# Attention scores on all 128 rows of TensorE in a two-layer decoder trunk, with four stages and the merge end in another order

## The chip, the cores and the metric

One core of a Trainium2 chip runs the whole program in one launch. The metric is the device time in microseconds of one execution. An execution with the profiler on is shown beside the timed ones.

## The reference

Two layers over `x` (512 tokens, 1024 channels), then an RMSNorm. In each layer `h = rmsnorm(x)` is projected once, and the columns are shared by three token mixers:

```python
...
scale = Dh ** -0.5
...
s = jnp.einsum('bqhd,bkhd->bhqk', qi, k, preferred_element_type=jnp.float32) * scale
s = s + ci[..., None] - c_keys[:, :, None, :]
...
prob = jax.nn.softmax(jnp.where(mask, s, NEG), axis=-1)
...
```

These lines are branch A (8 heads of 64, forget bias `c`, no rotation). Branch B has 8 rotated query heads that share 2 key groups, with a compressed, a selected (`sel`) and a window (`win`) part. Branch C has 4 heads of two rotated 64-wide maps each, whose probabilities are subtracted, and values of 128. Every branch result is gated, projected to 1024 channels, merged by sigmoid gates computed from `h`, projected once more and added to `x`. A gated per-layer embedding `p` is added last. Everything is float32.

## The kernel before

**Data.** Channels lie on partitions, tokens along the free axis. `hybrid_trunk` works through *tiles*: a tile is one projection of 128 output columns over 512 tokens. A float32 product is made of three products in a fast 32-bit format: `w_hi h_hi`, `w_lo h_hi`, `w_hi h_lo`, with `hi` the rounded value and `lo` the rest. `dense` (L732 to L734) issues these three for each k step of 128 channels. `hidden` (L745, L746) is the same for the compression tiles `w1k`, `w1v`, with two products of 256 columns a step and four steps a tile. For each tile ScalarE makes `w_hi` from `raw` (L1033) and VectorE `w_lo` (L1262). There are two buffers for them, four for `raw`, and two PSUM banks `D`: a tile can start only when the tile two before it is evacuated.

**Scores.** A stage handles one unit `u` (two heads, or two maps of a head) for the four query blocks `i`; its scores have `(i + 1) * 128` key columns. Stages 0 to 3 are branch A, 4 to 7 branch B (`sel` and `win`), 8 to 11 branch C. A head is 64 wide, so a pair of heads fills 128 partitions, head 0 on partitions 0 to 63, head 1 on the others. Item `S` makes both heads' scores in banks `Sc[0]` and `Sc[1]`:

```python
for step, (qx, kx) in enumerate(((q_hi[b], ka), (q_lo[b], ka), (q_hi[b], kb))):
    last = step == 2 and m != "a"
    for h in range(2):
        ps = slice(HD * h, HD * h + HD)
        ins = pe.matmul(Sc[h][:, 0:n], qx[ps, qs], kx[ps, 0:n], start=(step == 0), stop=last)
```

These are L879. In branch A one more product per head adds the forget bias from `ck` with the selector `selr` (L885). VectorE adds the mask and takes the maximum (L1514), ScalarE the exponential (L1148). Then TensorE transposes (`T`, L898) into `Tr`, one engine copies to `pT` (L540, L542), and TensorE multiplies with the values (`V`, L920). `N` normalizes on VectorE. In branch C `CB` combines the two maps, and `SQ`, `MS`, a power on POOL and `YN` make an RMS norm. `Y` transposes the unit's result (L936), and `YS` splits it into `y_hi` and `y_lo`.

**Queries and keys.** `qa` and `ka` go from the bank to high and low parts in the `arena` by one ScalarE copy (L1100) and one VectorE instruction (L1406), each on 128 partitions. `qb`, `ksb`, `kwb`, `qc`, `kc` are rotated: a copy to `qf` or `rx`, four DMAs that swap halves into `rs`, a product with the sine on POOL (`rs` to `rb`, L684), a product with the cosine, and at item `rot` the sum (L1503), the high part on ScalarE (L1141) and the low part on VectorE (L1505). `kcb` and `vcb` are laid out as `flat` for the `w1` tiles; `ht`, `kcmp`, `vcmp` finish the compression.

**Order.** `make_schedule` writes one list of items, and each engine walks through its share of it in that order. `dense_tiles` says by hand which tiles belong to which stage, and within a stage the k steps are spread evenly over the ticks of the attention work; some items follow a tile by a fixed count of steps (`rot` by 11, `ht` by 4). SP walks through the list too: its one DMA queue loads weights six tiles ahead and does the swaps. After stage 11 come 8 pairs `mgc`, `brc` (the merge), whose sums in `acc` are split into `h_hi` (L1173) and `h_lo` (L1605). Six parts are split ahead of the evacuation of the last `brc`, two behind it. Then come 8 tiles `out`, then `gate` and `ple`.

Of the kernel before, what the change touches and what calls it, by code (L numbers as in the profile page):

```python
# [32 lines left out]
P = 128  # L33
HD = 64
# [89 lines left out]
def make_schedule(NQ):  # L124
# [37 lines left out]
    def emit_group(g):  # L162
# [4 lines left out]
        if k == steps(kind) - 1:  # L167
# [13 lines left out]
            if kind == "w1k" and tiles[t][1] == 3:  # L181
                follow.extend([[4, ("ht", t)], [7, ("kcmp", t)]])
            if kind == "w1v" and tiles[t][1] == 3:
                follow.extend([[4, ("ht", t)], [7, ("vcmp", t)]])
# [88 lines left out]
def hybrid_trunk(nc, x, p, positions, norm_g, w_in, b_forget, cmp_pe_k, cmp_w1_k, cmp_b1_k, cmp_w2_k,  # L273
# [24 lines left out]
    for it in items:  # L298
# [14 lines left out]
        elif it[0] == "T":  # L313
            (pt_act if it[1] % 2 and branch(prob_rows[it[1]][0]) == "B" else pt_dve).add(it[1])
        elif it[0] == "YS":
            ysplit.add(it[1])
    DA0 = NM
# [11 lines left out]
    EARLY = 6  # L329
# [50 lines left out]
    with ctx:  # L380
# [21 lines left out]
        at_arena = -(-nc.sbuf_base // 32) * 32  # L402
        arena = sb("arena", [P, 16 * S], F32R)
        vbd = nc.alloc_sbuf_tensor_at("vbd", [P, 2, P], F32, offset=at_arena + 12 * S * 4)
# [3 lines left out]
        q_hi, q_lo = [part(0), part(1)], [part(2), part(3)]  # L408
        k_hi, k_lo = [part(4), part(5)], [part(6), part(7)]
        ks_hi, ks_lo, kw_hi, kw_lo = part(8), part(9), part(10), part(11)  # L410
# [17 lines left out]
        rb = sb("rb", [P, S])  # L428
# [24 lines left out]
        kcmpT = sb("kcmpT", [P, 2 * C32])  # L453
        cs_ = sb("cs_", [P, NQ, 2, C32])
# [8 lines left out]
        diag = rb  # L463
# [20 lines left out]
        def f(ap):  # L484
# [21 lines left out]
                 "act_flat").split()  # L506
        once = "nm_s npow_s diag_s pe_norm pe_rb lam_s act_lam lf_s p_ld zero_s xn_s vz_s va_step h2_hi_s h2_lo_s".split()
# [36 lines left out]
        def kind_of(t):  # L544
            if t < T0:
                return tiles[t][0]
            if t < T1:
                return ("mgc", "brc")[(t - T0) % 2]
# [9 lines left out]
        def rot_dst(kind, n):  # L558

            if kind == "ksb":  # L560
                return ks_hi, ks_lo, None
            if kind == "kwb":
                return kw_hi, kw_lo, None
            u = (4 if kind == "qb" else 8) + n
            return (k_hi[u % 2], k_lo[u % 2], u) if kind == "kc" else (q_hi[u % 2], q_lo[u % 2], u)

        with nc.Block() as block:

            @block.sync
            def _(sp):  # L570
# [12 lines left out]
                for L in range(DEPTH):  # L583
# [8 lines left out]
                    def static_load(t):  # L592
# [4 lines left out]
                        load(L, kind_of(t), tiles[t][1] if t < T0 else (t - T0) // 2 if t < T1 else t - T1 if t < T2 else (t - T2) // 2, t)  # L597
# [24 lines left out]
                    for it in items:  # L622
                        if it[0] == "end" and tiles[it[1]][0] in ROTATED:
# [4 lines left out]
                            if n > 1:  # L628
                                sp.wait_ge(M["pool_rot"], n - 1)
                            for a, b in ((0, 32), (32, 0), (64, 96), (96, 64)):  # L630
                                sp.dma_start(rs[a:a + 32, :], src[b:b + 32, :]).then_inc(M["sw_ld"], 16)  # L631
                        if it[0] == "end" and it[1] + 6 < T0 + 4:
                            static_load(it[1] + 6)

# [12 lines left out]
            def _(pool):  # L647
# [8 lines left out]
                pool.memset(halfs[:], -0.5).then_inc(i_const, 1)  # L656
                pool.memset(kcmpT[:], 0.0).then_inc(i_const, 1)
                pool.memset(f(ck[:]), 0.0).then_inc(i_const, 1)
                pool.wait_ge(i_const, 9)
# [5 lines left out]
                for n, r in enumerate((0, 32, HD, HD + 32)):  # L665
                    pool.affine_select(out=self_[:], in_=self_[:], compare_op=ALU.not_equal, fill=1.0, base=-r,
                                       pattern=[[-1, 8]], channel_multiplier=1).then_inc(i_const, 1)
                    pool.wait_ge(i_const, 12 + n)
                pool.tensor_copy(selr[:], self_[:]).then_inc(i_const, 1)
                for L in range(DEPTH):  # L670
# [5 lines left out]
                    for it in items:  # L676
                        if it[0] == "swap":
# [4 lines left out]
                            if n > 1:  # L682
                                pool.wait_ge(M["dve_rs"], n - 1)
                            pool.tensor_tensor(rb[:], rs[:], sinT[:], ALU.mult).then_inc(M["pool_rot"], 1)  # L684
                        if it[0] == "ht" and tiles[it[1]][0] == "w1v":
                            pool.wait_ge(M["pe_dense"], it[1] + 1)
# [1040 lines left out]
```

## Time and profile before

| | us |
|---|---|
| median of 3 runs | 1562.36 |
| lowest, highest | 1562.06, 1563.16 |
| profiled execution, its own time | 1562.81 |
| its span on the core | 1561.0 |
| TensorE busy (7957 products) | 1502.1 |
| VectorE busy | 941.8 |
| ScalarE busy | 638.4 |
| POOL busy | 74.0 |
| DMA | 129.47 MB, mean 83 GB/s |

The span is the time from the first to the last instruction of the core; the execution has 1.8 us more around it. Busy time is the union of the records of an engine, so overlapping products are counted once. A line of the profile names the source line, engine, operation, what is written and what is read. An idle time before a group is put down to the instruction that ended it. The second layer repeats the first one's pattern from about 768 us on.

### The profile page before, as it was taken

To read this page: it belongs to the slowest core of one execution; us is meant where nothing else is said; L and a number is where in the kernel's file an instruction comes from. 1 tells how busy PE (TensorE), PEld (TensorE's weight loads), DVE (VectorE), ACT (ScalarE), POOL (GpSimd) and SP (SyncE) were. 2 spreads that over 40 slices of the span, in tenths; PEclk is the share of its full clock that TensorE was granted. 3 is DMA by queue.
4 is the path that set the end of the run, shared out by engine and by line. 5 is a ranking of instruction groups with operands and counts; after the bars stand their busy time and mean duration, and the time that the engine had idled before them with its cause. 6 is when DMAs were issued, how large, how long until landed. Compare 5 with 4: busy or idle time off the path is not lost.

```text
span 1561.0 us, 22645 instructions
## 1 busy us (share of the span) xinstructions
PE 1502.1 (96%) x7957; PEld 1205.9 (77%) x7957; DVE 941.8 (60%) x2205; ACT 638.4 (41%) x1492; POOL 74.0 (5%) x80
## 2 busy tenths in 40 slices
PE   8999999999999999999999999999999999999997
PEld 6777777887787777878787777787887777788785
DVE  6866665555556766455576657655555666754544
ACT  6533434333344434343444334334333443433343
POOL 1000000000000000000200000000000000000011
PEclk9999999999999999999999999999999999999998
DMA  7223322222223332331342324222222333233222
GB/s 195 81 82 88 96 66 63 62 68 61 68 62 94 92 79 78 94 112 58 112 112 68 102 68 109 71 54 66 62 62 74 80 83 88 68 96 106 81 82 74
DMA packets 250299, 129.47 MB, mean 83 GB/s; under 512 B 45690, under 2 KB 245972, under 8 KB 250196
## 3 DMA queue, kind: packets, MB, share of 16 engines
q1 hardware_dynamic: 250196, 128.13, 30.8%
q8 instruction: 60, 0.98, 0.3%
q14 instruction: 43, 0.35, 0.1%
HBM read 118.67 MB, written 2.10 MB: 77 GB/s over the span
## 4 chain that ended last, share of the span: by engine, by line
PE 79%; DVE 9%; issue 5%; ACT 4%; DMA 1%; POOL 1%; SPq 1%; ACTq 0%; DVEq 0%; POOLq 0%
PE D L732 21%; PE D L734 19%; PE D L733 19%; PE Ob L920 7%; PE S L879 4%; PE T L898 3%; DVE w_lo L1262 2%; ACT w_hi L1033 1%; ACT probs L1148 1%; DMA rs<-rx 1%; PE Mb L936 1%; SPq L631 1%; DVE h_lo L1605 1%; PE Mb L846 1%; PE Ob L924 1%
## 5 line engine op out<-in xcount | busy, mean ns | idle before, releaser
L732 PE MATMUL D<-h_hi,w_hi 128*128 128x512 f32 x1264 | 543.1, 430 | 17.2 <-DVE zs L1410 4.8
L734 PE MATMUL D<-h_lo,w_hi 128*128 128x512 f32 x1264 | 496.5, 393 | 0.0
L733 PE MATMUL D<-h_hi,w_lo 128*128 128x512 f32 x1264 | 494.5, 391 | 0.0
L1262 DVE TENSOR_TENSOR w_lo<-raw,w_hi 128x512 fp32r<-128x512 f32 (+2 forms) x504 | 297.2, 631 | 313.7 <-ACT w_hi L1033 313.4
L1033 ACT ACTIVATE w_hi<-raw 128x512 fp32r<-128x512 f32 (+2 forms) x504 | 266.3, 575 | 313.9 <-PE D L734 313.0
L732 PEld LDWEIGHTS D<-h_hi,w_hi 128*128 128x128 f32 x1264 | 238.6, 189 | 78.1 <-issue 20.6
L1148 ACT ACTIVATE probs<-probs,nmax 128x128 f32<-128x128 f32 (+3 forms) x256 | 141.9, 555 | 366.7 <-DVE nmax L1514 366.7
L734 PEld LDWEIGHTS D<-h_lo,w_hi 128*128 128x128 f32 x1264 | 237.5, 188 | 53.0
L733 PEld LDWEIGHTS D<-h_hi,w_lo 128*128 128x128 f32 x1264 | 239.5, 189 | 30.7 <-issue 0.5
L1514 DVE CUSTOM_DVE_ANT_0 probs<-S,maskb 128x128 f32<-128x128 f32 (+3 forms) x256 | 115.1, 486 | 51.1 <-PE S L879 30.3
L542 DVE COPY pT<-T 128x128 f32<-128x128 f32 (+3 forms) x160 | 77.4, 486 | 50.1 <-PE T L898 49.6
L920 PEld LDWEIGHTS Ob<-v_b,pT 128*128 128x128 f32 x640 | 90.5, 190 | 12.3 <-ACT pT L540 1.9
L898 PE MATMUL T<-ident,probs 128*128 128x128 f32 x560 | 97.9, 273 | 1.7 <-ACT probs L1148 1.7
L879 PE MATMUL S<-arena 64*128 64x384 f32 (+3 forms) x768 | 93.8, 349 | 0.9 <-DVE arena L1406 0.9
L732 PE MATMUL D<-y_hi,w_hi 128*128 128x512 f32 x224 | 94.0, 420 | 0.4 <-DVE y_lo L1600 0.4
L898 PEld LDWEIGHTS T<-ident,probs 128*128 128x128 f32 x560 | 72.3, 140 | 28.0 <-ACT probs L1148 5.4
L879 PEld LDWEIGHTS S<-arena 64*128 64x128 f32 x768 | 57.0, 185 | 45.6 <-issue 41.3
L734 PE MATMUL D<-y_lo,w_hi 128*128 128x512 f32 x224 | 87.9, 393 | 0.0
L733 PE MATMUL D<-y_hi,w_lo 128*128 128x512 f32 x224 | 87.5, 390 | 0.0
L920 PE MATMUL Ob<-v_b,pT 128*128 128x64 f32 x640 | 85.4, 264 | 0.3
L684 POOL TENSOR_TENSOR rb<-rs,sinT 128x512 f32<-128x512 f32 x28 | 36.2, 1292 | 970.0 <-DMA rs<-rx 588.3
L920 PEld LDWEIGHTS Ob<-v_ac,pT 128*128 128x128 f32 x480 | 67.0, 192 | 16.1 <-DVE pT L542 8.9
(241 smaller groups left out, 1496.8 us busy)
## 6 DMA issues: line engine op xcount, KB each, us to landing
raw<-in_w_in_dram SPq DMA_DIRECT2D x124, 512.0 KB, 3.9
raw<-in_w_in_dram SPq DMA_DIRECT2D x32, 256.0 KB, 3.7
raw<-in_w_out_dram SPq DMA_DIRECT2D x16, 512.0 KB, 4.0
raw<-in_w_ple_gate_dram SPq DMA_DIRECT2D x16, 512.0 KB, 4.2
rs<-rx SPq DMA_DIRECT2D x80, 64.0 KB, 2.0
raw<-in_cmp_w_k_dram SPq DMA_DIRECT2D x8, 512.0 KB, 3.7
raw<-in_cmp_w_v_dram SPq DMA_DIRECT2D x8, 512.0 KB, 3.7
raw<-in_w_br_a_dram SPq DMA_DIRECT2D x16, 256.0 KB, 2.9
```

Of the source, the lines that this page charges most:

```text
L542: eng.tensor_copy(pT[:, k % 2, 0:n], Tr[k % 2][:, 0:n]).then_inc(M["pt_dve_s"], 1)
L684: pool.tensor_tensor(rb[:], rs[:], sinT[:], ALU.mult).then_inc(M["pool_rot"], 1)
L732: pe.matmul(o, w_hi[:, sl, cs], hi[:, k, :], start=(k == 0), stop=False)
L733: pe.matmul(o, w_lo[:, sl, cs], hi[:, k, :], start=False, stop=False)
L734: ins = pe.matmul(o, w_hi[:, sl, cs], lo[:, k, :], start=False, stop=last)
L879: ins = pe.matmul(Sc[h][:, 0:n], qx[ps, qs], kx[ps, 0:n], start=(step == 0), stop=last)
L898: ins = pe.transpose(Tr[k % 2][:, j * P:(j + 1) * P], src[:, j * P:(j + 1) * P], ident[:])
L920: ins = pe.matmul(Ob[:, oc], pT[:, k % 2, j * P:(j + 1) * P], vs(j), start=(j == 0), stop=(j == i))
L1033: A(w_hi[:, sl, half], raw[:, ring(L, t, RAW), half], ACT.Copy).then_inc(M["act_hi"], 1)
L1148: A(probs[:, r % NP_, 0:n], probs[:, r % NP_, 0:n], ACT.Exp, scale=-1.0, bias=nmax[:, r % 8:r % 8 + 1], accum_out=sums[:, u % 2, i, c:c + ...
L1262: TT(w_lo[:, sl, half], raw[:, ring(L, t, RAW), half], f(w_hi[:, sl, half]), ALU.subtract).then_inc(M["dve_lo"], 1)
L1514: dve.tensor_tensor_reduce(probs[:, r % NP_, 0:n], Sc[r % 2][:, 0:n], maskb[:, S - n:S], -1.0, 3.0e38, ALU.add, ALU.min, nmax[:, r % 8:r % ...
```

## The change

*Scores.* Queries and keys get another layout. For each head the stationary operand holds its high part on one half of the partitions and its low part on the other half (`q_st`). The moving operand holds the same key part on both halves, once for the high part and once for the low part (`k_hi`, `k_lo`, a set per key tile). A head's scores are two products on 128 rows, `q_st x k_hi` and `q_st x k_lo`. That adds `q_lo k_lo` to the three products of before. In branch A a third product with `selr` and `ck` on 128 rows follows. Head 0 comes first, then head 1, each with its own wait for `dve_max`.

*Making the layout.* Each evacuation and each rotation writes its high and its low part in two instructions of 64 partitions and 512 columns, in place of one of 128 partitions. Key parts are written on one half and copied to the other by two DMAs of 256 KB per key tile (10 key tiles per layer, semaphore `kd_s`). SP issues them, for `ka` at the tile's end and for the rotated ones at item `rot`, and waits there for VectorE. Scores wait for `kd_s`. `rb` is gone: POOL multiplies `rs` in place, and SP waits for `dve_rs` of the rotation before, not `pool_rot`, ahead of the swap. `vbd` has a place of its own and is cleared once.

*Stages -1 to 3.* The tiles stand in another order, and `ht` and `kcmp`/`vcmp` follow after 12 and 16 steps.

*Merge end.* The last four tiles are `mgc 6`, `mgc 7`, `brc 6`, `brc 7`; three `h` parts are split ahead of the sum of `brc 6`, five behind that of `brc 7`.

```diff
--- before.py
+++ after.py
...
-    st = {-1: [("va", 0), ("va", 1), ("va", 2), ("va", 3), ("fg", 0), ("qa", 0), ("ka", 0), ("qa", 1)]}
+    st = {-1: [("va", 0), ("va", 1), ("va", 2), ("va", 3), ("fg", 0), ("ka", 0), ("qa", 0), ("qa", 1)]}
     st[0] = [("kcb", 0), ("ka", 1), ("za", 0), ("w1k", 0)]
-    st[1] = [("qa", 2), ("ka", 2), ("w1k", 1), ("ksb", 0), ("w1k", 2), ("za", 1)]
-    st[2] = [("qa", 3), ("w1k", 3), ("ka", 3), ("za", 2), ("vcb", 0)]
-    st[3] = [("qb", 0), ("w1v", 0), ("kwb", 0), ("w1v", 1), ("za", 3), ("w1v", 2), ("vsb", 0), ("w1v", 3), ("vwb", 0)]
+    st[1] = [("qa", 2), ("w1k", 1), ("ka", 2), ("w1k", 2), ("za", 1), ("w1k", 3), ("vcb", 0)]
+    st[2] = [("qa", 3), ("w1v", 0), ("ka", 3), ("w1v", 1), ("za", 2), ("w1v", 2), ("qb", 0)]
+    st[3] = [("w1v", 3), ("ksb", 0), ("za", 3), ("kwb", 0), ("vsb", 0), ("vwb", 0)]
...
+        q_st = [[part(6 * b + h) for h in range(2)] for b in range(2)]
+        k_at = [2, 8, 12]
+        k_hi = [[part(a + 2 * h) for h in range(2)] for a in k_at]
+        k_lo = [[part(a + 2 * h + 1) for h in range(2)] for a in k_at]
+        KS, KW = 0, 2
...
                             if n > 1:
-                                sp.wait_ge(M["pool_rot"], n - 1)
+                                sp.wait_ge(M["dve_rs"], n - 1)
...
+                            if kind == "ka":
+                                sp.wait_ge(M["dve_evac"], dve_evac.after(it[1]))
+                            else:
+                                sp.wait_ge(M["qk_s"], rots.after(it[1]))
+                            if kdup.after(it[1]) > 1:
+                                sp.wait_ge(M["kd_s"], 32 * (kdup.after(it[1]) - 1))
+                            for h in range(2):
+                                both = part(k_at[k_set(kind, n)] + 2 * h, 2)
+                                sp.dma_start(f(both[half(1 - h), :]), f(both[half(h), :])).then_inc(M["kd_s"], 16)
...
+                            for h in range(2):
+                                if r >= 2:
+                                    pe.wait_ge(M["dve_max"], r - 1 + h)
+                                qx = q_st[b][h][:, i * P:n]
+                                pe.matmul(Sc[h][:, 0:n], qx, k_hi[ks][h][:, 0:n], start=True, stop=False)
+                                ins = pe.matmul(Sc[h][:, 0:n], qx, k_lo[ks][h][:, 0:n], start=False, stop=m != "a")
+                                if m == "a":
+                                    hh = 2 * u + h
+                                    ins = pe.matmul(Sc[h][:, 0:n], selr[:, hh:hh + 1].to_broadcast([P, P]), ck[:, 0:n],
+                                                    start=False, stop=True)
+                                ins.then_inc(M["pe_s"], 1)
...
-                                dst = (q_hi if kind == "qa" else k_hi)[n % 2]
-                                A(dst, D[:], ACT.Copy, scale=QSCALE if kind == "qa" else 1.0).then_inc(M["act_evac"], 1)
+                                dst = (q_st if kind == "qa" else k_hi)[n % 2]
+                                for h in range(2):
+                                    ins = A(dst[h][half(h), :], D[half(h), :], ACT.Copy, scale=QSCALE if kind == "qa" else 1.0)
+                                ins.then_inc(M["act_evac"], 1)
...
-                            A(hi_, rc[:], ACT.Copy).then_inc(M["act_rot"], 1)
...
+                            for h in range(2):
+                                ins = A(dst[h][half(h), :], rc[half(h), :], ACT.Copy)
+                            ins.then_inc(M["act_rot"], 1)
...
+                    lo(T1 - 2)
+                    lo(T1 - 1)
+                    for m in range(3):
                         merged_lo(m)
+                    merged_last(0)
+                    lo(T1)
+                    merged_last(1)
+                    for m in range(3, NM):
+                        merged_lo(m)
+                    lo(T1 + 1)
...
```

Where instructions stand. TensorE, a score group of 384 columns in stage 4 (`D` dense products, `S` scores, `T` transpositions), before:

```order
L733 MATMUL D<-h_hi,w_lo 128x512
L734 MATMUL D<-h_lo,w_hi 128x512
L879 MATMUL S<-arena 128x384 x6
L732 MATMUL D<-h_hi,w_hi 128x512
L733 MATMUL D<-h_hi,w_lo 128x512
L734 MATMUL D<-h_lo,w_hi 128x512
L898 MATMUL T<-ident,probs 128x128 x2
```

and now:

```order
L744 MATMUL D<-h_hi,w_lo 128x512
L745 MATMUL D<-h_lo,w_hi 128x512
L892 MATMUL S<-arena 128x384
L893 MATMUL S<-arena 128x384
L892 MATMUL S<-arena 128x384
L893 MATMUL S<-arena 128x384
L743 MATMUL D<-h_hi,w_hi 128x512
L744 MATMUL D<-h_hi,w_lo 128x512
L745 MATMUL D<-h_lo,w_hi 128x512
L910 MATMUL T<-ident,probs 128x128 x2
```

Six products on 64 rows, which one row counts together, became four on 128 rows; what is around them stands where it stood.

VectorE in stage 1, from the end of tile `ka 2` on, with a `w1` tile behind it on TensorE (`w_lo` are low weights, `arena` is the key's low part, `tmp` a `w1` tile's sum, `ISA probs` the mask and maximum), before:

```order
L1262 TENSOR_TENSOR w_lo<-raw,w_hi 128x512 x2
L1406 SCALAR_TENSOR_TENSOR arena<-D,arena 128x512
L1560 RECIPROCAL coef<-sums 128x2
L1561 TENSOR_TENSOR y_q<-Ob,coef 128x128
L1262 TENSOR_TENSOR w_lo<-raw,w_hi 128x512 x2
L1428 TENSOR_TENSOR tmp<-D,tmp 64x256
L1429 TENSOR_TENSOR tmp<-D,tmp 64x256
L1514 ISA probs,nmax<-S,maskb 128x384
```

and now:

```order
L1297 TENSOR_TENSOR w_lo<-raw,w_hi 128x512 x2
L1445 SCALAR_TENSOR_TENSOR arena<-D,arena 64x512 x2
L1604 RECIPROCAL coef<-sums 128x2
L1605 TENSOR_TENSOR y_q<-Ob,coef 128x128
L1558 ISA probs,nmax<-S,maskb 128x384
L1558 ISA nmax 128x1
L1558 ISA probs,nmax<-S,maskb 128x384
L1558 ISA nmax 128x1
L548 COPY pT<-T 128x256
```

The evacuation into `arena` is two instructions of 64 partitions; scores now stand ahead of the next low weights and the `w1` sum (`tmp`), which came first before.

VectorE in stage 9, between the combination of two maps and the norm of the unit before (`rc` and `arena` are the rotation of `qc 2`, `msq` and `y_q` the items `MS` and `YN`), before:

```order
L1528 SCALAR_TENSOR_TENSOR probs<-probs,coef 128x256
L1503 TENSOR_TENSOR rc<-rc,rb 128x512
L1505 TENSOR_TENSOR arena<-rc,arena 128x512
L542 COPY pT<-T 128x128
L1578 TENSOR_SCALAR msq<-msq 128x4
L1582 TENSOR_TENSOR msq<-msq 128x4
L1583 TENSOR_TENSOR msq<-msq 128x4
L1584 TENSOR_SCALAR msq<-msq 128x4
L1585 TENSOR_TENSOR msq<-msq 128x4
L1586 TENSOR_TENSOR y_q<-y_q,msq 128x512
```

and now:

```order
L1572 SCALAR_TENSOR_TENSOR probs<-probs,coef 128x256
L1540 TENSOR_TENSOR rc<-rc,rs 128x512
L1545 TENSOR_TENSOR arena<-rc,arena 64x512 x2
L548 COPY pT<-T 128x128
L1622 TENSOR_SCALAR msq<-msq 128x4
L1626 TENSOR_TENSOR msq<-msq 128x4
L1627 TENSOR_TENSOR msq<-msq 128x4
L1628 TENSOR_SCALAR msq<-msq 128x4
L1629 TENSOR_TENSOR msq<-msq 128x4
L1630 TENSOR_TENSOR y_q<-y_q,msq 128x512
```

The rotation stands where it stood, right ahead of `MS`, and its last step is two instructions.

## Rows read from the trace of the kernel before

**Rows 1.** The page, busy time, share of the span and instructions of each engine.
```profile
PE 1502.1 (96%) x7957; PEld 1205.9 (77%) x7957; DVE 941.8 (60%) x2205; ACT 638.4 (41%) x1492; POOL 74.0 (5%) x80
```

**Rows 2.** The waits: engine, line, releaser: us in total, times, longest us.
```profile
PEld D L732 <- DVE w_lo L1262: 14.1, 12, 2.5
PE Mb L936 <- DVE y_q L1586: 7.4, 6, 1.3
PE Mb L819 <- DVE tmp L1432: 4.6, 2, 2.3
```

**Rows 3.** The timeline, PE, around a score group of 512 columns, branch B.
```profile
315.67 0.40 PE L734 MATMUL D<-y_lo,w_hi 128*128 128x512 f32 x1
315.99 0.97 PE L879 MATMUL S<-arena 64*128 64x512 f32 x6
316.89 0.50 PE L732 MATMUL D<-h_hi,w_hi 128*128 128x512 f32 x1
317.23 0.40 PE L733 MATMUL D<-h_hi,w_lo 128*128 128x512 f32 x1
317.47 0.40 PE L734 MATMUL D<-h_lo,w_hi 128*128 128x512 f32 x1
```

**Rows 4.** The same, around groups of 384, 256 and 128 columns.
```profile
301.82 0.40 PE L734 MATMUL D<-h_lo,w_hi 128*128 128x512 f32 x1
303.21 0.39 PE L733 MATMUL D<-h_hi,w_lo 128*128 128x512 f32 x1
1173.02 0.40 PE L734 MATMUL D<-h_lo,w_hi 128*128 128x512 f32 x1
1174.23 0.40 PE L733 MATMUL D<-h_hi,w_lo 128*128 128x512 f32 x1
450.87 0.40 PE L734 MATMUL D<-y_lo,w_hi 128*128 128x512 f32 x1
452.02 0.39 PE L733 MATMUL D<-h_hi,w_lo 128*128 128x512 f32 x1
```

**Rows 5.** The timeline around tile `w1k 1`: PE, then ScalarE, then VectorE.
```profile
107.39 0.40 PE L734 MATMUL D<-h_lo,w_hi 128*128 128x512 f32 x1
107.62 0.28 PE L745 MATMUL D<-w_hi,arena 128*128 128x256 f32 x1
108.46 0.28 PE L746 MATMUL D<-w_lo,arena 128*128 128x256 f32 x1
110.59 0.47 PE L732 MATMUL D<-h_hi,w_hi 128*128 128x512 f32 x1 [0.96 <-DVE arena L1406]
108.94 0.58 ACT L1100 ACTIVATE arena<-D 128x512 fp32r<-128x512 f32 x1
109.77 0.68 DVE L1406 SCALAR_TENSOR_TENSOR arena<-D,arena 128x512 fp32r<-128x512 f32 x1
```

**Rows 6.** The timeline, PE: transpositions of 128 columns, two and three together.
```profile
303.67 0.38 PE L898 MATMUL T<-ident,probs 128*128 128x128 f32 x2
305.73 0.49 PE L898 MATMUL T<-ident,probs 128*128 128x128 f32 x3
```

**Rows 7.** The timeline, PE, at the end of the merge, seventh k step of `out 0`.
```profile
684.34 0.50 PE L732 MATMUL D<-h_hi,w_hi 128*128 128x512 f32 x1 [1.47 <-DVE h_lo L1605]
```

**Rows 8.** The timeline, PE, in stage 3, behind tile `w1v 2`.
```profile
197.75 0.47 PE L732 MATMUL D<-h_hi,w_hi 128*128 128x512 f32 x1 [2.31 <-DVE zs L1410]
```

**Rows 9.** A stretch: busy PE, PEld, DVE, ACT, POOL; then granted clock, DMA share, GB/s.
```profile
187.00:230.00 43.00, 39.86 (x229) 32.25 (x228) 26.71 (x69) 13.78 (x36) 1.61 (x2) 0.96 0.36 86
```

**Rows 10.** The timeline, ScalarE and PE, behind the rotation of `qb 1`.
```profile
243.19 0.36 ACT L540 ACTIVATE pT<-T 128x256 f32<-128x256 f32 x1
243.45 0.40 PE L734 MATMUL D<-h_lo,w_hi 128*128 128x512 f32 x1
243.68 0.58 PE L920 MATMUL Ob<-v_b,pT 128*128 128x64 f32 x4
```

**Rows 11.** The page, DMA issues: count, KB each, us to landing.
```profile
raw<-in_w_in_dram SPq DMA_DIRECT2D x32, 256.0 KB, 3.7
```

More of the change, by code:

```diff
@@ L316, in hybrid_trunk @@
             ysplit.add(it[1])
+    kdup = Count()
+    for it in items:
+        if it[0] == "end" and tiles[it[1]][0] == "ka" or it[0] == "rot" and tiles[it[1]][0] in ("ksb", "kwb", "kc"):
+            kdup.add(it[1])
     DA0 = NM
@@ L453, in hybrid_trunk @@
         kcmpT = sb("kcmpT", [P, 2 * C32])
+        vbd = sb("vbd", [P, 2, P])
         cs_ = sb("cs_", [P, NQ, 2, C32])
@@ L546, in kind_of @@
                 return tiles[t][0]
+            if t >= T1 - 4 and t < T1:
+                return ("mgc", "mgc", "brc", "brc")[t - T1 + 4]
             if t < T1:
@@ L633, in _ @@
                             static_load(it[1] + 6)
+                        if it[0] in ("end", "rot") and it[1] in kdup.order and (tiles[it[1]][0] == "ka") == (it[0] == "end"):
+                            kind, n, _ = tiles[it[1]]
+                            if kind == "ka":
[7 more added lines that the diff above has]
+                                sp.dma_start(f(both[half(1 - h), :]), f(both[half(h), :])).then_inc(M["kd_s"], 16)
                     sp.wait_ge(M["dve_ysplit"], 12)
@@ L681, in _ @@
                             pool.wait_ge(M["sw_ld"], 64 * n)
[L682 to L686, printed above, removed]
-                            pool.memset(vbd[:], 0.0).then_inc(M["vz_s"], 1)
+                            pool.tensor_tensor(rs[:], rs[:], sinT[:], ALU.mult).then_inc(M["pool_rot"], 1)
                         if it[0] == "MS":
@@ L882, in _ @@
-                            if m == "a":
-                                for h in range(2):
-                                    ps, hh = slice(HD * h, HD * h + HD), 2 * u + h
-                                    pe.matmul(Sc[h][:, 0:n], selr[ps, hh:hh + 1].to_broadcast([HD, P]), ck[ps, 0:n],
-                                              start=False, stop=True).then_inc(M["pe_s"], 1)
+                                    if u == 4:
+                                        pe.wait_ge(M["kd_s"], 32 * kdup.after(tile_of[("ksb", 0)]))
+                                elif u == 4:
+                                    pe.wait_ge(M["kd_s"], 32 * kdup.after(tile_of[("kwb", 0)]))
@@ L1605, in merged_lo @@
                         STT(h_lo[:, m, :], acc[:, m, :], 0.5, f(h_hi[:, m, :]), ALU.mult, ALU.subtract).then_inc(M["dve_merge"], 1)
-                    def merge_tiles(i, m0, last):
+                    with dve.Fori(0, NM // 2 - 1) as i:
                         for j in range(4):
-                            t = T0 + 2 * m0 + j
-                            if last and j == 3:
-                                for m in range(EARLY):
-                                    merged_lo(m)
+                            t = T0 + j
```

167 lines of the change are left out of this document (91 added, 76 removed).

## The prediction

> **What bounds the kernel now.** I read the busy times first: TensorE is busy for 96% of the span, VectorE for 60%, ScalarE for 41% [rows 1]. So an instruction taken off TensorE is worth its full time wherever TensorE is not waiting, and an instruction added on VectorE or ScalarE costs nothing until TensorE has to wait for it. Second, the waits: TensorE's are short and have few causes [rows 2]. It waits for VectorE's `y_q` before a `Y` transposition (7.4 us in 6 waits), for `tmp` before `ht` (4.6 us), and for low weight parts (14.1 us). Third, the timeline of TensorE around a score group. Records of products overlap, so the price of anything there is a distance between starts, not a recorded length: `D` products of 512 columns start 0.23 to 0.24 us apart and are recorded as 0.40 us long [rows 3].
>
> **The score products.** Before, a group is six products on 64 rows, the two heads in pairs. At 512 columns the last `D` before it starts at 315.67, the six scores at 315.99, the next `D` at 316.89 and the one after at 317.23 [rows 3]. From 315.67 to 317.23 is 1.56; two `D` distances are 0.46; so the group costs 1.10 us. Three rounds of 0.23 are only 0.69 of that. The rest is an entry gap (0.32 instead of 0.23) and a longer exit (0.33, then 0.34 to the next product). The pairs do run side by side: six products of 512 columns in 0.90 us is faster than one after the other. The same reckoning gives 0.93 at 384 columns (303.21 - 301.82 - 0.46), 0.75 at 256 (1174.23 - 1173.02 - 0.46) and 0.69 at 128 (452.02 - 450.87 - 0.46) [rows 4].
>
> After, a group is four products on 128 rows, one behind the other. At 512 columns I take the `D` distance, 0.23. At 256 columns the eight products of a `w1` tile start at 107.62 to 108.46, seven distances of 0.12 [rows 5]. At 128 columns the third transposition adds 0.49 - 0.38 = 0.11 [rows 6]. For 384 I take the value between, 0.17. That makes 0.92, 0.69, 0.48 and 0.44, if nothing is lost on entry or exit because `D` and `S` now are products of one shape and type. The gain is 0.18, 0.24, 0.27 and 0.25 per group. Of the 24 groups at 128 columns in branches B and C, 18 are followed by the compressed products, their transpositions or `V` and not by `D`; the long exit is not in their price, so I take 0.17 as their mean. Branches B and C have 24 groups of each width in both layers: (0.18 + 0.24 + 0.27 + 0.17) x 24 = 20.6 us. Branch A has 8 of each, with the `ck` row: one more round before, two more products now, so each gains one distance less: (0.25 - 0.11) + (0.27 - 0.12) + (0.24 - 0.17) + (0.18 - 0.23) = 0.31, x 8 = 2.5 us. **Together -23.1 us** on TensorE.
>
> The Trainium skill has two rules here. "TensorEngine Tiling (Array Packing)", Key Properties, says that changing the tiling mode drains the engine. By it the entry and exit gaps belong to the 64-row form and go with it; the trace agrees so far as it can, 0.32 into a score group against 0.23 from `D` to `V` [rows 3, 10]. The same list says that different tiles load and multiply in parallel; by that alone the change gives up concurrency, and that is a rival below.
>
> **Merge end.** The stall before the seventh k step of the first `out` tile, 1.47 us [rows 7], is `h_lo` part 6 standing on VectorE behind the low weights of `out 1` and the sum and add of the last `brc`. Now `mgc 6, mgc 7, brc 6, brc 7` leaves the sum of channel group 6 to run beside `brc 7`, and only that of 7 and five `h_lo` parts behind it. There VectorE has a fused sum and an add (about 1.3 us at 0.6 to 0.7 each) and the five parts at 0.7; TensorE has the transpositions of `p` (about 1 us) and eight k steps of 0.68. Part 7 is ready about 5.5 us behind `brc 7`, its k step due at 5.8. I count -1.7 us per layer, **-3.4**. Bounds: -4.0 (the stall and its short successor) and +1 (the second `out` tile's weights, split last, come late).
>
> **Stages 0 to 3.** `ht` moves 8 steps later: its 4.6 us of wait [rows 2] go. Tiles `w1` no longer stand behind a `rot`; the 2.31 us wait for `zs` [rows 8] and, I assume, one like it in the second layer, 4.6 together, shrink to about 0.3 each. But a `w1` tile is short, and the tile behind it needs the bank of the tile before it. Before, `ka 2` and `qa 3` stand so. There from the last product at 107.39 ScalarE copies at 108.94, VectorE subtracts at 109.77, and `D` goes on at 110.59, 3.2 us later [rows 5]. After, `qa 2`, `ka 2`, `qa 3` and `ka 3` all stand so, and both copies are in halves: half the partitions, the same 512 columns. I price a second half a little under the recorded 0.58 and 0.68 [rows 5], since records overlap: 0.5 on ScalarE and 0.6 on VectorE, so 4.3 us, of which `w1`, scores and one transposition cover 2.1 to 2.5: 2.2 + 1.8 us twice per layer, 8.0, beside 1.7 for the other `w1` tiles, 9.7 per layer, 19.4. Before it is 4.6 + 4.6 + about two thirds of the 14.1 for `w_lo` [rows 2], an estimate, 18.6. In the stretch with the 2.31 us wait TensorE's granted clock is 0.96 in the mean of 43 us [rows 9], so 1.7 us more were lost, which need not return. **Net -1**; bounds -12 (all short-tile waits vanish) and +8 (each is 1 us longer).
>
> **What the halves add.** 8 evacuations and 14 rotations per layer have a second ScalarE and a second VectorE half. Most are hidden beside `D` tiles of 5.5 us. Three places are not.
> - Behind the rotations of `qb 1` to `qb 3` and `qc 0`, ScalarE's copy of `pT` ends at 243.55 and `V` starts at 243.68 [rows 10]: no slack. A half more on ScalarE, 0.5, and scores that are 0.1 to 0.2 shorter ahead of it give 0.6 each, 8 times: +4.8.
> - Ahead of `MS` and `YN` in stages 9 and 10 the rotation of `qc` stands right before `MS` on VectorE, as the order shown above has it, and TensorE waits up to 1.3 for `y_q` [rows 2]. There the halves add 0.5 + 0.6, and the scores in between shorten by 0.24: +1.3 each, 4 times: +5.2.
> - At the start of stage 0 VectorE is the late one; two evacuations in halves less one copy of `ck` give +1.4 in the first layer and +0.5 in the second. In stage 11 and at transpositions that wait for the exponentials, the shorter scores only lengthen the wait: +2.
> **Together +13.9.** Bounds 0 and 28 (twice each).
>
> **The new transfers.** 40 DMAs of 256 KB copy each key half to the other half. A load of that size lands in 3.7 us [rows 11]. Between the end of a key tile and its first scores lie at least 3.4 us of `D` (for `kwb`, whose scores come two ticks later) and mostly 9 us and more, so I cost them at nothing; SP's waits for `qk_s` stand behind VectorE work that its next load waits for anyway. Should one be late, it is 1 to 3 us in a layer. POOL's product now overwrites `rs`, and SP waits for `dve_rs` before the next swap: the previous rotation's sum is 1 to 2 tiles old by then, cost nothing. `vbd` and `ck` save one memset and one copy.
>
> **Sum.** -23.1 - 3.4 - 1 + 13.9 = -13.6, from the profiled execution's 1562.8 us to 1549.2; its time is 0.45 us over the median, so I say **1549**.
>
> **Rivals.**
> - *Rows lost.* If the gaps around a score group come from its waits and its change of bank and not from the 64-row form, they stay, and each group has one more product time, in branch A two: (0.11 + 0.12 + 0.17 + 0.23) x (24 + 2 x 8) = 25.2 us more; with merge end and stages as above and 5 us of new waits left, 1562.4 + 25.2 - 4.4 + 5 = **1588**. It decides where the distance from `D` into `S` stays at 0.32. Against it: `V` also waits for a semaphore and changes the bank, and comes 0.23 behind `D` [rows 10]. Chance 0.1. By the skill's rule on independent tiles it would be this.
> - *Eaten up.* The halves cost twice what I take: 28 us, **1563**, within noise of before. For it: VectorE and ScalarE each work through one list in the order written, so an engine late at one place is late at the next, and VectorE's 60% [rows 1] is a mean. Chance 0.15.
> - *Slack holds.* VectorE and ScalarE take the halves where they idle, and the chains start earlier because scores end earlier: no new waits, **1535**. Chance 0.2. For it: ScalarE is 41% busy [rows 1].
> - The forecast, 1542 to 1556: chance 0.55.
>
> A difference under 0.2%, 3.1 us, is what a measurement of this kernel can hardly tell from none. Faster by more: 0.55 + 0.2 + a third of 0.15, 0.80. Within: 0.07. Slower: the first rival and the tail of the second, 0.13. The range holds all but that rival and the far tails: 1533 to 1566.
>
> **What would show it.** Steps right: the four score products start 0.23 apart at 512 columns, 0.32 is nowhere, and the first `D` behind a group is 0.23 before the second. The wait for `h_lo` and for `tmp` is gone; those for the evacuated `arena` and for `y_q` are longer. Wrong: score products of 128 columns more than 0.15 apart (weight loads of 128 rows not hidden); any wait of scores for a DMA; a wait for `y_q` no longer than before.

## The result and the profile after

The changed kernel takes 1576.63 us (median of 4 runs, 1576.19 to 1578.43), the kernel before 1562.76 beside it. The ratio is 1.0089, with a 95% interval of 1.0072 to 1.0107: **slower by 13.9 us**. The forecast was 13 us faster; the time lies outside the range.

The page of the changed kernel, busy times, the shares of the chain of waits, and the heaviest groups:

```profile
PE 1491.4 (95%) x7701; PEld 1245.1 (79%) x7701; DVE 974.8 (62%) x2247; ACT 668.7 (42%) x1536; POOL 73.5 (5%) x77
...
PE 74%; DVE 12%; ACT 7%; issue 5%; POOL 0%; DMA 0%; SPq 0%; ACTq 0%; DVEq 0%; POOLq 0%
...
L743 PE MATMUL D<-h_hi,w_hi 128*128 128x512 f32 x1264 | 538.9, 426 | 22.0 <-DVE arena L1445 10.2
...
arena<-arena SPq DMA_DIRECT2D x40, 256.0 KB, 3.6
```

Against [rows 1] TensorE is busy for 10.7 us less although the span is 13.4 longer (1574.4 us). In the chain PE fell from 79% to 74%, VectorE rose from 9% to 12% and ScalarE from 4% to 7%. TensorE did less and waited more.

TensorE's longest waits (us in total, times, longest):

```profile
PE Mb L948 <- DVE y_q L1630: 14.1, 6, 3.0
PE D L743 <- DVE arena L1445: 10.2, 6, 2.3
PE D L743 <- DVE arena L1442: 7.9, 4, 2.2
PE T L910 <- ACT probs L1179: 7.5, 12, 0.9
PE Ob L932 <- DVE pT L548: 7.0, 8, 1.8
...
PE Ob L932 <- ACT pT L546: 5.1, 6, 0.9
PE Mb L830 <- DVE y_f L1639: 3.0, 2, 1.8
```

`y_q` was 7.4 in six waits, 1.3 at most [rows 2]; now 14.1, up to 3.0. `arena` (evacuations of `ka`, `qa`) and the waits for ScalarE's `probs` and `pT` are new at this size. The wait for `tmp`, 4.6 in two [rows 2], is back under another name before the same `ht` transposition: 3.0 in two. There is no wait of `S` for a transfer.

The score group of 512 columns, TensorE's timeline, branch B:

```profile
318.66 0.39 PE L745 MATMUL D<-y_lo,w_hi 128*128 128x512 f32 x1
318.88 0.39 PE L892 MATMUL S<-arena 128*128 128x512 f32 x1
319.11 0.39 PE L893 MATMUL S<-arena 128*128 128x512 f32 x1
319.34 0.39 PE L892 MATMUL S<-arena 128*128 128x512 f32 x1
319.56 0.39 PE L893 MATMUL S<-arena 128*128 128x512 f32 x1
319.79 0.39 PE L743 MATMUL D<-h_hi,w_hi 128*128 128x512 f32 x1
320.02 0.39 PE L744 MATMUL D<-h_hi,w_lo 128*128 128x512 f32 x1
```

The starts are 0.22 to 0.23 us apart throughout. From the last `D` before the group to the second `D` behind it are 1.36 us; less two `D` distances the group costs 0.90 to 0.91 (1.10 before [rows 3]). The forecast said 0.92. The 0.32 is gone.

Stages 9 and 10 show the loss. The timeline of VectorE, ScalarE and TensorE of the changed kernel around `y_q` in stage 10:

```profile
555.49 0.69 DVE L1540 TENSOR_TENSOR rc<-rc,rs 128x512 f32<-128x512 f32 x1
557.57 1.39 DVE L1545 TENSOR_TENSOR arena<-rc,arena 64x512 fp32r<-64x512 f32 x2 [1.39 <-ACT arena L1171]
558.88 0.28 DVE L548 COPY pT<-T 128x128 f32<-128x128 f32 x1
559.18 0.17 DVE L1622 TENSOR_SCALAR msq<-msq 128x4 f32<-128x4 f32 x1
...
561.27 0.69 DVE L1630 TENSOR_TENSOR y_q<-y_q,msq 128x512 f32<-128x512 f32 x1
...
556.26 1.27 ACT L1171 ACTIVATE arena<-rc 64x512 fp32r<-64x512 f32 x2 [1.42 <-issue]
...
558.76 0.39 PE L745 MATMUL D<-h_lo,w_hi 128*128 128x512 f32 x1
562.10 1.08 PE L948 MATMUL Mb<-ident,y_q 128*128 128x128 f32 x4 [2.96 <-DVE y_q L1630]
```

and the same place in stage 9 by windows (busy PE, its instructions, granted clock, DMA share, GB/s):

```profile
501.00:514.00 13.00, 13.00 (x68) 1.00 0.32 83
514.00:518.00 4.00, 1.33 (x7) 0.97 0.26 65
518.00:521.50 3.50, 3.16 (x10) 0.55 0.01 4
```

The same instructions of the kernel before, in stage 10:

```profile
552.01 0.68 DVE L1503 TENSOR_TENSOR rc<-rc,rb 128x512 f32<-128x512 f32 x1
552.78 0.63 ACT L1141 ACTIVATE arena<-rc 128x512 fp32r<-128x512 f32 x1 [1.42 <-issue]
553.45 0.69 DVE L1505 TENSOR_TENSOR arena<-rc,arena 128x512 fp32r<-128x512 f32 x1 [0.75 <-ACT arena L1141]
556.33 0.69 DVE L1586 TENSOR_TENSOR y_q<-y_q,msq 128x512 f32<-128x512 f32 x1
557.16 0.63 PE L936 MATMUL Mb<-ident,y_q 128*128 128x128 f32 x4 [1.32 <-DVE y_q L1586]
```

Two halves take 1.27 us on ScalarE and 1.39 on VectorE, where one instruction of 128 rows took 0.63 and 0.69: half the partitions, the same time. VectorE waits 1.39 for ScalarE's two and then does its own two. From the rotation's sum to `y_q` it is 5.78 us (555.49 to 561.27) where it was 4.32 (552.01 to 556.33), 1.46 more, and TensorE's wait is 2.96 instead of 1.32. Behind such a wait TensorE can run for 3.4 us at 1.2 GHz instead of 2.4, as here in stage 9. In the body of the program (25 us to 1515 us) there is one such stretch before and there are seven after, 23.9 us in all. At half clock each costs half its length, 1.7 us: 11.9 instead of 1.7. The Trainium skill, "TensorE: Matmul & The Clock Gate", Terms, reckons the penalty as throttled time times one minus the clock's share, which is this half; a run below agrees.

### The profile page after: what moved, and what is told of

Read it like the earlier page. It is cut to its first block, busy times and chain, and to the rows that moved or that the text cites. A ratio compares the mean times of both kernels' runs of the same rounds, so it can differ in the third digit from the quotient of the medians.

```text
span 1574.4 us, 22204 instructions
## 1 busy us (share of the span) xinstructions
PE 1491.4 (95%) x7701; PEld 1245.1 (79%) x7701; DVE 974.8 (62%) x2247; ACT 668.7 (42%) x1536; POOL 73.5 (5%) x77
## 4 chain that ended last, share of the span: by engine, by line
PE 74%; DVE 12%; ACT 7%; issue 5%; POOL 0%; DMA 0%; SPq 0%; ACTq 0%; DVEq 0%; POOLq 0%
PE D L743 20%; PE D L745 19%; PE D L744 19%; PE Ob L932 6%; PE T L910 3%; DVE w_lo L1297 3%; ACT w_hi L1057 2%; PE S L893 2%; ACT probs L1179 2%; PE S L892 2%; ACT arena L1171 1%; ACT arena L1125 1%; DVE probs L1558 1%; DVE arena L1442 1%; PE Mb L948 1%
## 5 line engine op out<-in xcount | busy, mean ns | idle before, releaser
L743 PE MATMUL D<-h_hi,w_hi 128*128 128x512 f32 x1264 | 538.9, 426 | 22.0 <-DVE arena L1445 10.2
L698 POOL TENSOR_TENSOR rs<-rs,sinT 128x512 f32<-128x512 f32 x28 | 36.5, 1304 | 1006.3 <-DMA rs<-qf 589.5
L892 PE MATMUL S<-arena 128*128 128x128 f32 (+3 forms) x256 | 78.5, 316 | 2.3 <-DVE arena L1442 2.3
L893 PE MATMUL S<-arena 128*128 128x128 f32 (+3 forms) x256 | 80.2, 322 | 0.0
```

The source lines that it names most:

```text
L743: pe.matmul(o, w_hi[:, sl, cs], hi[:, k, :], start=(k == 0), stop=False)
L892: pe.matmul(Sc[h][:, 0:n], qx, k_hi[ks][h][:, 0:n], start=True, stop=False)
L893: ins = pe.matmul(Sc[h][:, 0:n], qx, k_lo[ks][h][:, 0:n], start=False, stop=m != "a")
```

## The experiments

Times are medians; a difference from the kernel before is what the ratio makes of 1562.8 us, one between two other kernels is that of their medians, which were not measured side by side. Where a stage is spoken of, its first score product is laid beside the same one of another trace.

**e1_merge.** The kernel before with the new end of the merge alone.

```diff
+            if t >= T1 - 4 and t < T1:
+                return ("mgc", "mgc", "brc", "brc")[t - T1 + 4]
```

> The kernel before with the merge end alone in the new order. My theory, that the halves of evacuations and rotations and the clock dips behind their waits ate the gain, has this part as it was forecast: 3 to 4 us faster, 1559, the wait for h_lo gone. The rival theory that a reordered end gives its gain back at the next tiles expects 0 to 1 us.

1560.19 us, ratio 0.9982 (0.9972 to 0.9992): -2.8. The wait for `h_lo` is gone; each layer ends about 2 us earlier against its stage 11, while this trace has two stretches at half clock where the kernel before has one. The term -3.4 holds.

**e2_order.** The kernel before with the new order of stages -1 to 3 and the later `ht` and `kcmp`, `vcmp`.

```diff
-    st[1] = [("qa", 2), ("ka", 2), ("w1k", 1), ("ksb", 0), ("w1k", 2), ("za", 1)]
+    st[1] = [("qa", 2), ("w1k", 1), ("ka", 2), ("w1k", 2), ("za", 1), ("w1k", 3), ("vcb", 0)]
-                follow.extend([[4, ("ht", t)], [7, ("kcmp", t)]])
+                follow.extend([[12, ("ht", t)], [16, ("kcmp", t)]])
```

> The kernel before with the new order of stages -1 to 3 and the later ht, kcmp and vcmp alone, without halves. My theory: the waits for tmp and for zs go and the bank waits behind four query and key tiles cost 1 us each as they do now: 3 us faster (0 to 6). The rival theory, that the order itself is what costs (stages 0 to 3 of the changed kernel are 5 us behind before when the shorter scores are counted), expects 4 to 8 us slower.

1552.34, ratio 0.9936 (0.992 to 0.9953): **-10**. The expectation had 0 to 6, its rival the other sign: both missed. By the start of stage 4 it is 7.2 us ahead in the first layer (211.2 against 218.3) and 4.7 more in the second. Counted from start to start, TensorE's waits over 0.3 us in stages 0 to 3 are 22.0 us in both layers before and 12.0 here. The one stretch at half clock, in stage 3, is gone too; another in stage 11 of the second layer takes that back. TensorE behind the short tiles `w1k 1` and `w1k 2`:

```profile
103.47 0.47 PE L732 MATMUL D<-h_hi,w_hi 128*128 128x512 f32 x1 [0.88 <-DVE arena L1408]
113.15 0.47 PE L732 MATMUL D<-h_hi,w_hi 128*128 128x512 f32 x1 [0.53 <-DVE arena L1408]
```

With undivided evacuations these waits are 0.9 and 0.5, and the `ht` transposition, which waited for `tmp`, has none. In the changed kernel the same two are

```profile
106.93 0.47 PE L743 MATMUL D<-h_hi,w_hi 128*128 128x512 f32 x1 [2.19 <-DVE arena L1442]
119.50 0.47 PE L743 MATMUL D<-h_hi,w_hi 128*128 128x512 f32 x1 [1.88 <-DVE arena L1445]
```

1.3 more each, a half on ScalarE and one on VectorE.

**e3_halves.** The kernel before; evacuations of `qa`, `ka` and the two last steps of every rotation written as two instructions of 64 partitions.

```diff
-                            A(hi_, rc[:], ACT.Copy).then_inc(M["act_rot"], 1)
+                            for h in range(2):
+                                ins = A(hi_[half(h), :], rc[half(h), :], ACT.Copy)
+                            ins.then_inc(M["act_rot"], 1)
```

> The kernel before with each query and key evacuation and each rotation's last step written in two instructions of 64 partitions, and nothing else: the results are those of before. My theory: 15 to 25 us slower (1578 to 1587), TensorE waits for arena, pT, the exponentials and y_q grow as in the changed kernel, and stretches at the lower clock appear behind the longer waits. The rival theory, that the halves hide and the faster scores made the waits, expects under 6 us.

1611.34, ratio 1.0325 (1.0304 to 1.0346): **+51** (+48.4 against the median beside it, the number that later expectations use). The expectation had 15 to 25. This is over three times the term of +13.9, and more than the whole loss of the change. There are eight stretches at half clock (13.6 us lost) against one.

**e4_scores.** The kernel before with two products on 128 rows per head, on operands as they lie. The scores mix the two heads.

```diff
-                            for step, (qx, kx) in enumerate(((q_hi[b], ka), (q_lo[b], ka), (q_hi[b], kb))):
+                            for h in range(2):
+                                pe.matmul(Sc[h][:, 0:n], qx, ka[:, 0:n], start=True, stop=False)
+                                ins = pe.matmul(Sc[h][:, 0:n], qx, kb[:, 0:n], start=False, stop=m != "a")
```

> The kernel before with two products of 128 rows per head in the places of the three of 64 rows, on the operands as they lie, so the two heads are mixed in the scores: only the time is of use. No halves, no new transfers. My theory: 23 us less on TensorE, a fifth of it lost in longer waits, 1544 (1541 to 1548). The rival theory, that every microsecond taken from the scores only lengthens waits, expects 1552 or more.

1544.76, ratio 0.9884 (0.9868 to 0.9901): -18, as expected. The rival that rows are lost falls. The 128 groups of the changed kernel, each reckoned as the one above, cost 94.7 us in all, those before 117.0, so 22 us are saved on TensorE; some 4 of them go into waits that shorter scores only lengthen and one more stretch at half clock.

**e5_evac, e6_rot.** The diff of e3_halves split: its evacuations alone, its rotations alone.

> The kernel before, with only the eight evacuations of qa and ka per layer written in two 64-row instructions on ScalarE and on VectorE. The halves of all 22 tiles per layer cost 48 us in e3_halves, 44 pairs in two layers, 1.1 us for each. Theory A (every half is paid in full, wherever it stands, because ScalarE and VectorE work through chains that TensorE waits for): 16 pairs, +17.6 us, 1580. Theory B (the bank of the tile before is what counts, and the evacuations hold it; rotations cost only at the places of the forecast, +10): +38 us, 1601. Theory C (most of it is the copy of the rotations ahead of pT and exponentials): under +8 us, 1570.

> The kernel before, with only the copies and subtractions at the end of the 14 rotations per layer in two 64-row instructions. Theory A: 28 pairs at 1.1 us, +31 us, 1593. Theory B: +10 us, 1573. Theory C: over +40 us, 1603. If e5 and e6 together give clearly less than the 48 us of e3_halves, what one delays the other delays again, and there is no price for one half.

1581.97, ratio 1.0124 (1.01 to 1.0148), and 1599.23, ratio 1.0226 (1.0203 to 1.025): +19 and +35, for 16 and 28 pairs, 1.2 and 1.3 us each: by the totals theory A is the nearest. But e5_evac has four stretches at half clock and e6_rot ten, against one before, 5 and 15 us. Without them a pair costs 0.9 and 0.7 us, where its two added instructions last 1.3 together. So not every half is paid in full. In the first layer of e6_rot the stages 4 to 8 are 0.8 to 1.1 longer each, and 9 and 10 3.2. That 3.2 is 1.6 more of wait for `y_q` (3.06 beyond the normal distance of starts in stage 10, 1.48 before) and one stretch at half clock, 1.7.

**e7_no_halves.** The diffs of e1, e2 and e4 together, heads mixed in the scores as there; no halves, no transfers.

> The kernel before with the new merge end, the new order of stages and two 128-row products per head on the operands as they lie (the heads are mixed in the scores, the rest of the computation is whole); no half instructions, no transfers. The three parts alone gave -2.8, -10.4 and -18.0 us. If they add up: 1531.5. If the order's and the scores' gains are the same waits: 1538 to 1542. The distance from here to the changed kernel (1576.6) is what halves and transfers cost in the new order: 45 us if they cost there what halves alone cost in the old one.

1531.75, ratio 0.9797 (0.9775 to 0.9819): -32 where the parts alone sum to -31 (-2.8 - 10 - 18); they add up. The halves and the transfers together cost 44.9 us in the new order (1576.63 - 1531.75). First score products of the stages (us from the start of each timeline) say where:

```
stage        before   e7_no_halves   changed   e9_in_place
0              63.9       64.2         65.9       66.1
1              90.8       91.0         93.5       94.1
4             218.3      211.4        222.2      214.2
8             451.2      438.3        452.9      441.5
9             492.4      478.8        494.2      482.1
11            575.9      560.8        582.1      564.2
0, layer 2    830.8      814.0        839.2      819.1
```

**e10_transfers.** The changed kernel with undivided instructions into the first buffers, its 40 transfers of 256 KB and their waits kept. The heads are mixed in the scores here too, and the low parts of queries are not used.

```diff
-                            for h in range(2):
-                                ins = A(dst[h][half(h), :], rc[half(h), :], ACT.Copy)
-                            ins.then_inc(M["act_rot"], 1)
+                            A(dst[0], rc[:], ACT.Copy).then_inc(M["act_rot"], 1)
```

> The changed kernel without its halves: one 128-row instruction for high and one for low parts into the first buffer, its two transfers of 256 KB per key tile at their places with their waits; scores of both heads read the first buffers (heads are mixed in the scores and the low parts of queries not used as they should be, the rest is whole). If the transfers are hidden, as the sum had it: e7_no_halves, 1531.8, within 1.5 us. If they are part of the 45 us between e7_no_halves and the changed kernel: that part shows here, and e9_in_place can't be near 1536.

1531.81, ratio 0.9787 (0.9768 to 0.9807), e7_no_halves to 0.1 us by the medians and to 1.6 by the ratios, whose intervals overlap. The transfers cost nothing that can be measured, as the sum had it; the 44.9 us are the halves'.

**e11_act, e12_dve.** e3_halves with the halves on one engine only.

> The kernel before, halves on ScalarE alone (44 more instructions of 0.6 us in two layers, VectorE's in one). Halves on both cost 48.4 us. If the two stand one behind the other in the chain high part, low part, what follows: the ScalarE part is 0.6 / 1.3 of it, 20 to 24 us, and e11 and e12 add up to 48. If only one engine is late: one of them gives nearly all and the other nearly nothing.

> The kernel before, halves on VectorE alone (44 more instructions of 0.69 us in two layers). Chain theory: 24 to 28 us. One late engine: nearly all of 48 or nearly nothing. VectorE is the busier one (60%), and what waits behind its low part (MS, scores' maxima, w_lo) is waited for by TensorE, so if only one matters I say it is this.

1591.94, ratio 1.0166 (1.0145 to 1.0187), and 1593.0, ratio 1.0189 (1.0161 to 1.0217): +26 and +30. Each is 2 us over the range of the chain theory and together they are 56 against 51, but both engines count about alike; that one alone is late is refuted. Each trace has eight lengths of 3.4 us at half clock against one before, 12 us of its loss. By place they differ. In stages 4 and 5 the VectorE halves cost 0.0 and the ScalarE halves 0.8, in front of `pT` as the forecast had it; in stage 7 the VectorE halves cost nothing either. ScalarE behind the rotation of `qb 1` in e11_act, then TensorE:

```profile
247.91 1.25 ACT L1147 ACTIVATE arena<-rc 64x512 fp32r<-64x512 f32 x2
249.19 0.38 ACT L540 ACTIVATE pT<-T 128x256 f32<-128x256 f32 x1
248.69 0.40 PE L737 MATMUL D<-h_lo,w_hi 128*128 128x512 f32 x1
249.63 0.55 PE L923 MATMUL Ob<-v_b,pT 128*128 128x64 f32 x3 [0.54 <-ACT pT L540]
```

`V` now starts 0.94 behind the last `D`; it was 0.23 [rows 10]. e11_act also holds a clean price of the clock. Its waits for `y_q` in stages 9 and 10, and the windows around them:

```profile
525.08 0.63 PE L939 MATMUL Mb<-ident,y_q 128*128 128x128 f32 x4 [1.97 <-DVE y_q L1593]
567.47 0.63 PE L939 MATMUL Mb<-ident,y_q 128*128 128x128 f32 x4 [1.96 <-DVE y_q L1593]
```

```profile
521.00:526.00 5.00, 3.03 (x18) 1.00 0.22 55
567.50:572.50 5.00, 5.00 (x18) 0.66 0.24 66
```

The same wait twice, once with the clock whole and once with 3.4 us at half. Stage 9 is 0.65 us longer than in the kernel before, stage 10 is 2.21 longer: 1.56 for the clock, near the 1.7 reckoned above.

**e8_staged.** The changed kernel's computation with undivided instructions into `rs` and `rc`; four transfers per tile put the pieces into the stacked queries and doubled keys.

```diff
-                            for h in range(2):
-                                ins = A(dst[h][half(h), :], rc[half(h), :], ACT.Copy)
+                            A(rs.bitcast(F32R), rc, ACT.Copy).then_inc(M["act_rot"], 1)
+                            for h in range(2):
+                                for g in range(2):
+                                    sp.dma_start(dst, src).then_inc(M["kd_s"], 16)
```

> The changed kernel with the same computation, but high and low parts again made by one 128-row instruction each (except the two tiles of stage 0), into rs and rc, and the stacked queries and doubled keys built from these by four transfers per tile (128 KB each for queries, 256 KB for keys). 160 instructions of 64 rows become 80 of 128. If the halves are the cause and transfers stay hidden: 1576.6 - 40 x 1.1 = 1533. If transfers come late or disturb the weight loads: 1545 to 1565, with waits of S for arena by DMA. If the transfers and not the halves were what cost in the changed kernel: 1580 or more, since there are now twice as many.

1567.08, ratio 1.0019 (1.0004 to 1.0034): only 9.6 us better than the change, where 1533 was expected, or 1545 to 1565 with late transfers. In its trace stages 4, 5, 9 and 10 of the first layer are as long as in e7_no_halves to 0.03 us. Of the 32 us by which its span is longer, 29 are lost in stages 3, 7 and 8 of the two layers. About 14 of the 32 are the clock: nine lengths of 3.4 us at half clock against one. VectorE in stage 3, then the wait's total, count and longest:

```profile
186.56 0.69 DVE L1477 TENSOR_TENSOR rsc<-rx,cosT 128x512 f32<-128x512 f32 x1 [4.24 <-DMA arena<-rsc]
```

```profile
DVE rsc L1477 <- DMA arena<-rsc: 40.2, 12, 5.7
```

(`rsc` is `rs` and `rc` together.) The next rotation's first product goes into `rc` while the transfers still read it. A transfer that costs no engine time still holds its source until it has landed, and here the source was the buffer needed next.

**e9_in_place.** So the source must be where the result belongs. High parts go undivided into the first buffer of the pair, low parts into the second; SP puts the halves right in steps, five k steps apart, with 1 KB per partition to spare. `qa 0`, `ka 0` and `kwb 0`, whose scores come soon, keep halves.

```diff
+    HALVES = (("qa", 0), ("ka", 0), ("kwb", 0))
+                                step_ = [[(spare[top, :], q1[top, 0:S // 2]), (spare[low, :], q1[top, S // 2:S])],
+                                         [(q1[top, :], q0[low, :])],
+                                         [(q0[low, 0:S // 2], spare[top, :]), (q0[low, S // 2:S], spare[low, :])]][j]
+                                    step_ = [[(k1[top, :], k0[low, :]), (k1[low, :], k0[low, :])], [(k0[low, :], k0[top, :])]][j]
```

> The changed kernel's computation. In e8_staged all that was lost against e7_no_halves (32.8 us) fell in five places: VectorE waited 3.5 to 4.2 us for the four transfers out of rc before it could start the next rotation in rc (stages 3, 7 and 8 of both layers), and elsewhere the drift was 0.0. Here nothing is staged in rs or rc: one 128-row instruction each writes high parts into the first query (key) buffer and low parts into its second, and SP puts the halves right in two or three steps of transfers, five k steps apart, so that no engine waits for them; only qa 0, ka 0 and kwb 0 keep halves. If it is the halves: e7_no_halves plus 3 or 4 us for these three tiles and the start, 1536. If transfers disturb what runs beside them, whatever waits for them: over 1550.

1537.57 (5 runs, 1535.61 to 1540.41), ratio 0.9823 (0.9805 to 0.9842): 27 us faster than before, 39 than the change, and nothing of the computation is left out or mixed. Its page, its heaviest wait, and one of the scores:

```profile
PE 1479.8 (96%) x7701; PEld 1235.7 (81%) x7701; DVE 947.5 (62%) x2209; ACT 642.0 (42%) x1498; POOL 74.3 (5%) x77
...
PE 80%; DVE 9%; ACT 5%; issue 4%; DMA 0%; POOL 0%; SPq 0%; ACTq 0%; DVEq 0%; POOLq 0%
...
arena<-arena SPq DMA_DIRECT2D x56, 256.0 KB, 3.4
...
PE Mb L973 <- DVE y_q L1663: 8.3, 6, 1.5
...
PE S L917 <- issue: 3.1, 5, 1.0
```

The profile names nothing for the last wait. It stands before the first scores of stages 1, 9 and 10, and each of its five times ends within 0.1 us of the last landing of a transfer between buffers. So the transfers, two or three steps in a row, come a little late there, 3.1 us in all. No stretch at half clock is left in the body. By the table it is 3.1 us behind e7_no_halves at stage 1, where `ka 0` and `qa 0` with their halves have passed, 3.4 at stage 11, and 5.1 after the same tiles of the second layer. Adding the halves costs 45 to 51 us, and taking them out of the changed kernel, all but those of three tiles per layer, gives 39 back: shown in both directions.

## Why the prediction was wrong

- **The score products: right.** Forecast -23.1; the groups are 22 us cheaper, -18 in time alone. The price at each width held (0.92 forecast, 0.90 to 0.91 measured at 512). The rival *rows lost* falls. Of the two rules of the Trainium skill ("TensorEngine Tiling (Array Packing)", Key Properties) the one on draining fits: the entry gap of 0.32 went with the 64-row form. The one on independent tiles decides nothing here.
- **Merge end: right.** -3.4, measured -2.8.
- **The new transfers: right.** Nothing, measured 0.1, and no wait of `S` for one.
- **Stages 0 to 3: mis-sized, in part for the halves.** I forecast -1 for order and halves together. The order alone gives -10, and the sum without its 8.8 for the halves had -9.8. That this agrees is in part luck. The 14.1 us for `w_lo` [rows 2] stand under `PEld`, the weight loads, which overlap the products; the products themselves wait for `w_lo` only 1.9 us (`PE D L732 <- DVE w_lo L1262: 1.9, 8, 0.2`). Yet two thirds of the 14.1 stood in the sum as TensorE's loss before. Waits for `arena` (3.7) and `rx` (2.7) that I did not count make up for most of it. The waits behind short tiles I had right for the changed kernel: forecast 2.2 + 1.8 twice per layer, 8.0; measured 2.36, 2.04, 1.92 and 2.03 beyond the normal distance, 8.35. Two things I missed. That the 4.6 us of wait of `ht` go holds only without halves: with them the `ht` transposition waits 3.0 us again in the two layers. And the clock fell in stage 1 of both, 3.4 us.
- **What the halves add: the step that failed.** Together with the 1.1 in each of the four short-tile waits per layer (8.8) my sum had 22.7 us for them; they cost 44.9. By place, changed kernel against e7_no_halves, both layers, forecast in brackets: start 1.7 (1.4), stages 0 to 3 18.1 (8.8), 4 to 7 8.2 (4.8), 8 1.8 (0), 9 and 10 10.4 (5.2), 11 with the start of the next layer 4.0 (2.5). Of the 22 us missing, **10.2 are the clock**: six stretches more at half clock, two in stages 0 to 3, three in 9 and 10, one net in 11. I had read the clock (0.96 in one stretch [rows 9]) and used it only for a loss that "need not return"; that longer waits bring new ones stood in no term. (The one in stage 11 came behind a wait for `pT` of 1.8 us that is as long before and brought none there.) Without it stages 9 and 10 are 5.3 against 5.2 and stage 11 is 2.3 against 2.5, so those waits were sized right. The other 12 us, found by subtraction, are halves taken as hidden or priced too low. A second half lasts 0.63 and 0.69 where I took 0.5 and 0.6, and by the stages in which the time is lost "most are hidden beside `D` tiles of 5.5 us" was wrong for `ksb`, `kwb`, `qb 0`, `qc 1` and `kc`. In e6_rot stages 2 and 3, which had no term for rotations, cost 10.8 us, 5.1 of them clock.
- *Eaten up*, the rival with the halves at twice the size, was the right mechanism and the right factor for the halves alone (44.9 is twice 22.7), but I doubled only the 13.9 and gave it 0.15. *Slack holds* argued from 41% of ScalarE. e11_act shows that this mean does not decide it: 44 more instructions of 0.63 us, 28 us of ScalarE's time, cost 26 us.

The sum with the measured terms: -2.8 - 10 - 18 + 44.9 = +14.1, against 13.9. The 44.9 is itself taken from the changed kernel, so this shows only that the other three add up.

## What to carry to other kernels

The instructions that were split by partitions here took twice the time, not the same. In a chain that passes from ScalarE to VectorE to TensorE, price each added instruction in full unless a row shows the receiver idle on something else for longer: the 44 pairs cost 1.0 us each, 0.8 without the clock, of the 1.3 that a pair lasts. Where the sum lengthens TensorE's waits, add a term for the clock: here it was 10 of 45 us. Where data have to change partitions, write them undivided and let transfers move them, early enough and out of a buffer that nobody needs next.

## What was not expected of the hardware

- Behind waits of TensorE of 2.0 to 3.2 us (start to start, beyond the normal distance) it ran for 3.4 us at 1.2 GHz seven times in the changed kernel; e6_rot has ten such stretches, the body of e9_in_place none. The wait does not settle it. Of the changed kernel's four waits of 2.96 to 3.00 us for `y_q` three were followed by such a stretch and the last was not, and the waits of 1.96 and 1.97 us in e11_act went one way and the other. What decides between them no run here shows.
- 64 partitions cost ScalarE 0.63 us and VectorE 0.69 us per 512 columns, as 128 do.
- 56 more transfers of 256 KB and the small ones beside them (152.8 MB moved in e9_in_place, 129.5 before) left the loads' time to landing at 3.9 us.
